# A two-layer hybrid mixer block on Trainium2: GpSimd forms the rests of the opening, and the input is scaled one stage later

## The reference, cut to what matters

```python
for l in range(DEPTH):                      # DEPTH = 2
    mod = jax.nn.silu(c) @ w_ada[l] + b_ada[l]
    mod_c = jax.nn.silu(c_ctx) @ w_ada[l] + b_ada[l]
    sh1, sc1, g1, sh2, sc2, g2 = jnp.split(mod[:, None, :], 6, axis=-1)
    csh1, csc1, cg1, csh2, csc2, cg2 = jnp.split(mod_c, 6)
    y, yc = hybrid_mixer(x * (1 + sc1) + sh1, ctx * (1 + csc1) + csh1, ...)
    x = layer_norm(DEEPNORM_ALPHA * x + g1 * y, ln1_g[l], ln1_b[l])
    x = layer_norm(DEEPNORM_ALPHA * x + g2 * swiglu(x * (1 + sc2) + sh2, ...), ln2_g[l], ln2_b[l])
    ...                                     # the same for ctx, except in the last layer
```

## Time and profile before

| what | us |
|---|---|
| median of 3 runs | 3281.9 |
| lowest and highest | 3279.8, 3283.09 |
| the profiled execution's own time | 3276.59 |
| its span in the trace | 3274.8 |
| TensorE busy | 3091.9 (94%) |
| VectorE busy | 2163.4 (66%) |
| ScalarE busy | 1181.9 (36%) |
| GpSimd busy | 1483.1 (45%) |

### The profile page before, as it was taken

The page is one execution under the profiler, slowest core; times in us unless marked ns, Lnnn a source line. Parts: engine busy times, 40 slices in busy tenths (PEclk is TensorE's granted clock), DMA queues, the critical chain, the costliest instruction groups (busy, mean ns, idle before and its releaser), DMA issues. The chain is left out here.

```text
span 3274.8 us, 43633 instructions
## 1 busy us (share of the span) xinstructions
PE 3091.9 (94%) x16570; PEld 2625.1 (80%) x16570; DVE 2163.4 (66%) x3294; ACT 1181.9 (36%) x2273; POOL 1483.1 (45%) x1151
## 2 busy tenths in 40 slices
PE   4999989899999999999998999999899999999997
PEld 3798878688778888888886789878787778887886
DVE  8757977685676666645667467947776575555556
ACT  5267742361432222221113347742443323222113
POOL 0544222354434445445555464213454455555665
PEclk9999999999999999999999999999999999999999
DMA  8200042003222433425331200031022222224331
GB/s 330 97 8 1 1 141 71 15 27 129 65 83 71 140 127 126 140 81 206 125 112 49 90 8 1 1 123 33 17 94 78 80 88 78 84 90 155 99 94 65
DMA packets 96175, 280.13 MB, mean 86 GB/s; under 512 B 8416, under 2 KB 21856, under 8 KB 94560
## 3 DMA queue, kind: packets, MB, share of 16 engines
q1 hardware_dynamic: 91264, 257.42, 23.0%
q10 hardware_dynamic: 4704, 19.92, 1.5%
HBM read 224.89 MB, written 52.43 MB: 85 GB/s over the span
## 5 line engine op out<-in xcount | busy, mean ns | idle before, releaser
L3990 DVE SCALAR_TENSOR_TENSOR x_res<-ps,mod,x_res 128x512 f32<-128x512 f32 (+1 forms) x448 | 308.1, 689 | 234.8 <-PE ps L215 233.9
L3395 POOL TENSOR_TENSOR h_a_lo<-f_wraw,h_a_hi 128x512 fp32r<-128x512 f32 x126 | 183.7, 1474 | 390.8 <-ACT h_a_hi L3390 390.8
L213 PE MATMUL ps<-f_ahi,f_whi 128*128 128x512 f32 (+1 forms) x896 | 341.5, 381 | 11.6 <-DVE x_res L3990 8.8
L214 PE MATMUL ps<-f_alo,f_whi 128*128 128x512 f32 (+1 forms) x896 | 328.3, 366 | 0.0
L215 PE MATMUL ps<-f_ahi,f_wlo 128*128 128x512 f32 (+1 forms) x896 | 328.1, 366 | 0.0
L214 PE MATMUL ps<-h_lo,h_a_hi 128*128 128x512 f32 (+1 forms) x720 | 250.1, 347 | 0.0
L213 PEld LDWEIGHTS ps<-f_ahi,f_whi 128*128 128x128 f32 x896 | 169.8, 190 | 51.9 <-DVE x_res L3990 12.5
L213 PE MATMUL ps<-h_hi,whic 128*128 128x512 f32 (+1 forms) x544 | 199.0, 366 | 7.8 <-DVE wloc L466 7.8
L3746 POOL TENSOR_TENSOR f_alo<-f_gated,f_ahi 128x512 fp32r<-128x512 f32 (+1 forms) x95 | 120.2, 1282 | 180.7 <-ACT f_ahi L3936 179.6
L214 PE MATMUL ps<-h_lo,whic 128*128 128x512 f32 (+1 forms) x544 | 196.8, 362 | 0.0
L215 PE MATMUL ps<-h_hi,wloc 128*128 128x512 f32 (+1 forms) x544 | 196.6, 361 | 0.0
(11 more groups left out here) (397 smaller groups left out, 8976.7 us busy)
## 6 DMA issues: line engine op xcount, KB each, us to landing
f_wraw<-in_w_ffn SPq DMA_DIRECT2D x130, 512.0 KB, 4.5
ada_w<-in_w_ada SPq DMA_DIRECT2D x56, 512.0 KB, 5.9
h_hi_f<-in_w_ada SPq DMA_DIRECT2D x56, 512.0 KB, 4.1
o_wraw<-in_w_out SPq DMA_DIRECT2D x28, 512.0 KB, 3.6
act_spill<-f_gated SPq DMA_DIRECT2D x20, 640.0 KB, 3.4
f_gated<-act_spill SPq DMA_DIRECT2D x19, 640.0 KB, 5.2
wrawc<-in_w_in SPq DMA_DIRECT2D x22, 512.0 KB, 3.6
x_spill<-x_res ACTq DMA_DIRECT2D x16, 640.0 KB, 5.5
```

What stands on the lines that cost most here:

```text
L213: pe.matmul(out, w_hi, h_hi, start=first, stop=False)
L214: pe.matmul(out, w_hi, h_lo, start=False, stop=False)
L3395: pool.tensor_tensor(self.flat(self.lo[f]), src, raw(self.flat(self.hi[f])), ALU.subtract) \
L3990: dve.scalar_tensor_tensor(out=x, in0=pl.bank(down_bank(i) + d % 2, tn), scalar=pl.mod[:, G2 + n, who:who + 1], in1=x, op0=ALU.mult, op1=A ...
```

## The change

The rests of the modulated input (eight subtractions of 128x1280) are formed by GpSimd, ahead of its weight rests, and no longer by VectorE. ScalarE no longer scales x in the opening, doesn't store it, and doesn't wait for a store. The output projection of layer 0 loads x from the kernel's input tensor xT instead of x_spill. There ScalarE scales the loaded x in place, in four parts behind the early chunks' roundings and in a fifth behind the late chunk's, and VectorE waits for four scalings before its first eviction and for the fifth before the late ones.

```diff
--- before.py
+++ after.py
@@ -356,8 +356,8 @@
     tmp = [pl.at(f"modt{s}", [P, TOK], F32, kb=148 + 5 * s) for s in range(3)]
     order = [tile for k in range(KT) for tile in (SH1 + k, SC1 + k)]
     x_in = [pl.sem(f"open_x_in{k}") for k in range(KT)]
-    consts_in, spilled, plus_one, biased, scaled, rounded, kept, rest = (pl.sem(f"open_{x}") for x in (
-        "consts_in", "spilled", "plus_one", "biased", "scaled", "rounded", "kept", "rest"))
+    consts_in, plus_one, biased, scaled, rounded, rest = (pl.sem(f"open_{x}") for x in (
+        "consts_in", "plus_one", "biased", "scaled", "rounded", "rest"))
 
     def sync(sp, ring_loads):
         ada.start(sp)
@@ -384,11 +384,6 @@
                 if c == 0:
                     dve.wait_ge(done, n + 1)
 
-        def rest_of(k):
-            dve.wait_ge(rounded, k + 1)
-            dve.tensor_tensor(pl.lo[:, k, :], tmp[k % 3][:, :], raw(pl.hi[:, k, :]), ALU.subtract) \
-                .then_inc(rest, 1)
-
         dve.wait_ge(ada.bias_in, 16)
         dve.tensor_scalar(pl.bada[:, SC1:SC1 + KT], pl.bada[:, SC1:SC1 + KT], 1.0, None, ALU.add) \
             .then_inc(plus_one, 1)
@@ -401,11 +396,8 @@
             part = pl.mod[:, SH1 + k:SC1 + k + 1:KT, :]
             bias = pl.bada[:, SH1 + k:SC1 + k + 1:KT].unsqueeze(2).broadcast_to([P, 2, 2])
             dve.tensor_tensor(part, part, bias, ALU.add).then_inc(biased, 1)
-            if k >= 1:
-                rest_of(k - 1)
             if k == 2:
                 between()
-        rest_of(KT - 1)
         dve.wait_ge(consts_in, 16)
 
     def scalar(act, between):
@@ -421,14 +413,16 @@
                                scale=pl.mod[:, SC1 + k, who:who + 1]).then_inc(scaled, 1)
             act.wait_ge(scaled, 2 * k + 2)
             act.activation(pl.hi[:, k, :], tmp[k % 3][:, :], ACT.Copy).then_inc(rounded, 1)
-            act.activation(pl.x[:, k, :], pl.x[:, k, :], ACT.Copy, scale=ALPHA).then_inc(kept, 1)
-            act.wait_ge(kept, k + 1)
-            act.dma_start(pl.x_dram[:, k, :], pl.x[:, k, :]).then_inc(spilled, 16)
             if k == 0:
                 between()
-        act.wait_ge(spilled, KT * 16)
-
-    return Lead({c: [(rest, KT)] for c in range(3)}, lambda pe: None, scalar, vector, sync=sync, tiles_in=rest,
+
+    def gpsimd(pool):
+        for k in range(KT):
+            pool.wait_ge(rounded, k + 1)
+            pool.tensor_tensor(pl.lo[:, k, :], tmp[k % 3][:, :], raw(pl.hi[:, k, :]), ALU.subtract) \
+                .then_inc(rest, 1)
+
+    return Lead({c: [(rest, KT)] for c in range(3)}, lambda pe: None, scalar, vector, gpsimd, sync=sync, tiles_in=rest,
                 ada=ada)
 
 
@@ -616,6 +610,7 @@
 
     def gpsimd(self, pool):
         pool.sem_inc(self.ring.ready, 2)
+        self.lead.gpsimd(pool)
         self.rests(pool)
         self.split_values(pool)
 
@@ -2279,6 +2274,7 @@
     full = {c: sem(f"full{c}") for c in early + late}
     taken = {c: sem(f"taken{c}") for c in early + late}
     rooted, inverted, x_in, x_late_in = sem("rooted"), sem("inverted"), sem("x_in"), sem("x_late_in")
+    x_scaled = sem("x_scaled")
     normed, turned, rounded, rest = ([sem(f"{x}{p}") for p in range(2)]
                                      for x in ("normed", "turned", "rounded", "rest"))
     next_in = [sem(f"next_in{s}") for s in range(2)]
@@ -2323,7 +2319,8 @@
             load(0)
             load(1)
             def load_x(tiles_in, cols, signal):
-                sp.dma_start(pl.x[:, tiles_in, cols], pl.x_dram[:, tiles_in, cols]).then_inc(signal, 16)
+                source = a["xT"] if l == 0 else pl.x_dram
+                sp.dma_start(pl.x[:, tiles_in, cols], source[:, tiles_in, cols]).then_inc(signal, 16)
             load_x(slice(0, 2), slice(0, width), x_in)
             load_x(slice(6, 8), slice(0, width), x_in)
 
@@ -2457,6 +2454,13 @@
                     act.wait_ge(turned[p], n + 1)
                     act.activation(pl.hi[:, k, t0:t0 + tn], pl.bank(gather_bank(p, n), tn), ACT.Copy,
                                    scale=1.0 if k < 4 else gnorm(k)).then_inc(rounded[p], 1)
+                if l == 0:
+
+                    act.wait_ge(*((x_late_in, 16) if p else (x_in, 16 * (2 + len(early)))))
+                    for k0, k1, t0, t1 in ((2, 6, 512, SEQ),) if p else ((0, 2, 0, TOK), (6, 8, 0, TOK),
+                                                                         (2, 6, 0, 512), (2, 6, SEQ, TOK)):
+                        part = pl.x[:, k0:k1, t0:t1]
+                        act.activation(part, part, ACT.Copy, scale=ALPHA).then_inc(x_scaled, 1)
             act.wait_ge(next_in[0], 16)
             act.activation(ffn.hi[0][:, :], ffn.early[0][:, :], ACT.Copy).then_inc(next_rounded, 1)
             def round_late(p):
@@ -2527,6 +2531,8 @@
                 rest_of(0, n)
             norm.factors(dve)
             dve.wait_ge(x_in, 16 * (2 + len(early)))
+            if l == 0:
+                dve.wait_ge(x_scaled, 4)
             for m in range(KT):
                 if m < 4:
                     divide(tiles_of[1][m])
@@ -2544,6 +2550,8 @@
                     step(dve, c, k)
 
             dve.wait_ge(x_late_in, 16)
+            if l == 0:
+                dve.wait_ge(x_scaled, 5)
             evict(KT)
             for c in early:
                 norm.centre(dve, c)
```

## The result

The changed kernel takes 3288.8 us, the median of 20 runs (3283.99 to 3295.39); the kernel before, run beside it, takes 3279.7 us (20 runs, 3275.53 to 3283.09). The ratio is 1.0029, 95% interval 1.0023 to 1.0036, which is +9.5 us (+7.5 to +11.8). The prediction was 3288.9, as 7.0 us over a kernel before of 3281.9. The profiled execution took 3295.39 us, the slowest of the 20, with a span of 3293.6 us; the one before had 3276.59 and 3274.8.

What follows compares the result with a forecast made beforehand. VectorE was taken to pace the opening, where TensorE waits. Slower rests, less what the opening's end gives back, made +7.0 us, other edits 0: 3283.6 on the profiled execution, 3288.9 on the median of 3281.9; range 3281.5 to 3295.5.

Steps and rivals of the forecast that it cites:

- VectorE paces the opening, the transfers don't: Opening: VectorE sets the pace at 6.6 us per tile, 1.4 of it the rest; DMA engines nearly full but not waited for.
- 2.5 us per rest on GpSimd: Opening: each rest moved to GpSimd holds VectorE's products up by 2.5 us, against 1.4 on VectorE.
- The last biasing: VectorE's biasing of tile 7 in the opening: moves by +8.6 us, to about 69.9.
- The last rest at 76.6: Opening, tile 7: asked for at 73.1, waits 0.6 us, takes 2.9 on GpSimd; ends 10.5 us later than before.
- Block 2 at 83.1, or 84.8 with tile 7 at the lower clock: TensorE's start of weight block 2: +6.8 us, or +8.5 with tile 7 at 1.2 GHz, some then saved in block 2.
- The store's wait at about 1 us: End of the opening: removing the spill that ScalarE waited for is worth about 1 us of block 2's start.
- The projection at nothing: Layer 0's output projection: loading x and the added scalings cost 0, bounds 0 to +4 us, with 4 us of cover.
- A: Opening: VectorE keeps its pace without the rests, nothing lost to GpSimd; -8.5 us, 3273.4; chance 0.07.
- B: Layer 0's output projection pays as well, by late x loads or scalings: +3.5 us more, 3292.4; chance 0.05.
- D: VectorE's later sums, stretched and started later, become what ends the opening stage: +10 us, 3292; chance 0.05.
- C: Opening: smaller delay, GpSimd finds VectorE's gaps and the clock stays at its upper level: +3.5 us, 3285.4; chance 0.07.
- the stages behind the opening: Stages after the opening: no cost included in the sum; layer 0's projection, the only one examined, was put at 0.

Runs made afterwards that it cites:

- rests_back_on_vector: The changed kernel with its eight rests back on VectorE, x still neither scaled nor stored in the opening: 3276.55 us, ratio 0.9991.
- context_product_from_psum: The changed kernel with the opening's products for c_ctx reading their condition from PSUM instead of SBUF: 3274.76 us, ratio 0.9983.
- psum_order: context_product_from_psum with the PSUM products of neighbouring tiles side by side and the biasing between them on ScalarE: 3271.03 us, ratio 0.998.
- before_again: The kernel before, unchanged, run for a second profile: a single execution of 3275.93 us.
- after_again: The changed kernel, with nothing further changed, run for a second profile: 3287.95 us, ratio 1.0026.
- psum_order_last_on_vector: psum_order with the last rest, of tile 7, moved back from GpSimd to VectorE: 3268.94 us, ratio 0.9967.

## Why the prediction was right

- **VectorE paces the opening, the transfers don't.** Right. With 5.2 MB of stores gone and the rests on VectorE the biasings didn't move (61.26).
- **2.5 us per rest on GpSimd.** Right: 2.57 us of stretch in the mean of seven, 2.60 at most. The last biasing came at 70.50 for 69.9; seven rests at 2.57 instead of 2.5 are 0.5 of the 0.6.
- **The last rest at 76.6.** It ended at 77.7. It was asked for at 73.81 instead of 73.1, for the most part by the later biasing, and it waited 1.2 us for the running product, of which I had taken 0.6.
- **Block 2 at 83.1, or 84.8 with tile 7 at the lower clock.** It was the second in the first profile (85.41) and the first in the second (83.71); both 0.6 us later than written, since the last rest was 1.1 us late and TensorE started 2.4 us behind the start of GpSimd's weight rest, where I had taken 3.1. The lower clock at tile 7 was paid back at block 2, as foreseen: the stage was 7.0 us longer, and 6.0 (140.7 against 134.6) in the second pair.
- **The store's wait at about 1 us.** Right: 1.0 and 1.6 us against the two profiles of before. The other part of what rests_back_on_vector gained at block 2 is tile 6's clock and a shorter weight rest.
- **The projection at nothing.** Right: VectorE's evictions were late and TensorE didn't wait; from the stage's first activation (o_rs) to the rounding of the next weights (f_whi) it is 85.9 us in the kernel before and 86.0 in the changed one's second profile. Without the scalings all three profiles have 85.9; with them four of seven have 85.8 to 86.0 and three have 86.7 to 87.6, the first of the changed kernel among them. TensorE's idle time in that stretch is 3.1 to 3.6 us in all ten, so the three are longer in its busy time, at a granted clock of 0.97 or 0.98 instead of 0.99, and not by a wait.
- **Rivals.** A (no exclusion) fell with the first stretched product; B fell with the projection's idle time just given; D fell because the sums end at 132.8 us, 8 us ahead of TensorE. C fell because a gap of VectorE lets a rest start, but the next product then waits for its whole length; with tile 7 and block 2 at the upper clock (the second profile) the stage was still 6.0 us longer.

The mechanism is right, the size nearly so: 7.0 us were forecast, just under the interval of the 9.5 measured (7.5 to 11.8). That the absolute time agrees to 0.1 us is luck: the median of three that the forecast started from, 3281.9, lies 2.2 us above that of 20 runs, and the change was taken some 2 us too small; the two errors cancel. The term that the forecast had wrong is the one that it put at nothing, the stages behind the opening: layer 1's sums of states cost 1.7 us in both profiles of the changed kernel. The opening's own traces give 5.3 to 7.7 us (142.4 or 140.7 against 135.3 or 134.6), and the two together 7.0 to 9.4. Whether more is lost elsewhere is not settled; spells of the lower clock move single executions by more than that. Of the 20 runs of the changed kernel the fastest had a mean clock of 0.981 and the slowest 0.977.

## What to carry to other kernels

Before giving work of a loaded VectorE to GpSimd, look in the trace for one VectorE instruction of the same kind under a GpSimd instruction. If it is stretched by nearly GpSimd's whole length, the move costs that much, here 2.6 us for what took 1.4. The exclusion can be scheduled around: it spares instructions with an operand in PSUM, so two free banks, an order in which GpSimd's instruction falls on those, the biasing on ScalarE and the last rest back on VectorE turned +9.5 us into -10.8; of these, -3.0 come already with the rests left on VectorE, by taking the stores out and moving the scaling. Look at untouched stages too, in two profiles of each kernel: what comes back in both is a cost (1.7 us here), what doesn't may be chance. And in a trace in which the clock changes, split a difference into what the clock took and what a wait took before giving it to the wait.

## What the runs showed of the hardware

- A VectorE product with one input in PSUM kept 1.212 to 1.226 us in all 32 cases of context_product_from_psum and psum_order, of which 18 lay beside a rest; a biasing of four columns with both inputs in SBUF waited 1.3 us.
- Gaps of 0.03 to 0.14 us between dependent VectorE instructions (51.09 to 51.12 and 74.99 to 75.13 in the changed kernel) were enough for GpSimd to get its turn. The Trainium skill (SBUF — State Buffer, section "SBUF: two separate sides") says that whichever starts first holds the pair for the whole instruction; the trace agrees: a rest of 2.9 us stretched a product by up to 2.6 us, and each further element of the rest by 2.1 ns.
- The attention stage has two lengths, 259.2 to 259.4 and 263.5 to 263.8 us, in two profiles of the same kernel too, with the granted clock (0.98 and 0.97) as the visible difference.
- TensorE's gap ahead of block 2 does not alone tell the clock behind it. It was 0.50 over the next 4.6 us after gaps of 4.6 us (before) and 3.3 us (before_again); after gaps of 2.3 to 2.4 us it was 1.00 in after_again, rests_back_on_vector and psum_order, and 0.65 and 0.63 in context_product_from_psum and psum_order_last_on_vector.
